# An earlier request for one weight block, and no meeting point between the recurrent mixer and the output products

## The reference, cut to what matters

```
h = rmsnorm(x, g_mix);  z = h @ w_in
q, k, v, f   = z's fox columns          # forgetting attention, 8 heads of 64
zr           = z's recurrent columns    # token shift, then a delta-rule recurrence, 8 heads of 64
zg           = z's gate columns, 2048
y_fox  = fox_attention(q, k, v, log_sigmoid(f))                    # [1024, 512]
y_rwkv = (group_norm(rwkv_scan(...)) + bonus) * g                  # [1024, 512]
merged = sigmoid(zg[:1024]) * (y_fox  @ w_o_fox)
       + sigmoid(zg[1024:]) * (y_rwkv @ w_o_rwkv)
x = x + merged @ w_out
h2 = rmsnorm(x, g_ffn); ... convolved, gated feed-forward of width 2816 ...
x = x + sigmoid(rmsnorm(x, g_ple) @ w_ple_gate) * (p @ w_ple_up)
```

## Time and profile before

| | |
|---|---|
| median of 3 runs | 4171.37 us (4163.51 to 4181.7) |
| the profiled execution | 4164.4 us, its span 4162.7 us |
| TensorE busy (matmul) | 3855.2 us, 93% |
| VectorE busy | 2273.4 us, 55% |
| ScalarE busy | 1195.5 us, 29% |
| GpSimd busy | 448.0 us, 11% |
| mean granted TensorE clock | 0.955 |

### The profile page before, as it was taken

One profiled execution on the slowest core, in us unless ns is written; L12 is line 12 of the kernel. 1 busy time (PEld: TensorE's weight loads), 2 busy tenths in 40 slices (PEclk: granted clock), 3 DMA queues, 4 the chain that ended last, 5 costly groups with the idle time before them and its releaser, 6 DMA issues. The chain is left out here.

```text
span 4162.7 us, 76117 instructions
## 1 busy us (share of the span) xinstructions
PE 3855.2 (93%) x33370; PEld 3166.3 (76%) x33370; DVE 2273.4 (55%) x3787; ACT 1195.5 (29%) x1698; POOL 448.0 (11%) x440
## 2 busy tenths in 40 slices
PE   6999969888999999999999999788788999999998
PEld 5888847777877888888798677566676788888887
DVE  4643335555434666766625333466554476666675
ACT  4221234433222433121401322243323321111123
POOL 0001102231000433000000000232311000000000
PEclk9999979998999999999999999888889999999999
DMA  5221130113112334422233422201004211111112
GB/s 182 83 64 49 48 112 6 33 31 128 51 56 86 107 107 137 167 100 73 90 121 117 144 76 86 80 23 59 23 30 155 91 51 41 51 43 59 41 61 81
DMA packets 230589, 327.11 MB, mean 79 GB/s; under 512 B 17372, under 2 KB 171740, under 8 KB 230132
## 3 DMA queue, kind: packets, MB, share of 16 engines
q1 hardware_dynamic: 201616, 259.52, 18.8%
q10 hardware_dynamic: 28644, 62.72, 3.9%
HBM read 239.66 MB, written 82.54 MB: 77 GB/s over the span
## 5 line engine op out<-in xcount | busy, mean ns | idle before, releaser
L471 PE MATMUL ps<-sb_a_h,sb_whi 128*128 128x512 f32 (+1 forms) x2336 | 930.8, 398 | 5.1 <-DVE sb_wlo L432 5.1
L473 PE MATMUL ps<-sb_a_h,sb_whi 128*128 128x512 f32 (+1 forms) x2336 | 914.3, 391 | 0.0
L472 PE MATMUL ps<-sb_a_h,sb_wlo 128*128 128x512 f32 (+1 forms) x2336 | 914.2, 391 | 0.0
L471 PEld LDWEIGHTS ps<-sb_a_h,sb_whi 128*128 128x128 f32 (+1 forms) x2336 | 440.8, 189 | 113.0 <-issue 15.7
L472 PEld LDWEIGHTS ps<-sb_a_h,sb_wlo 128*128 128x128 f32 (+1 forms) x2336 | 441.0, 189 | 94.9 <-issue 4.9
L473 PEld LDWEIGHTS ps<-sb_a_h,sb_whi 128*128 128x128 f32 (+1 forms) x2336 | 440.5, 189 | 94.4
L422 ACT ACTIVATE sb_whi<-sb_wraw 128x2048 fp32r<-128x2048 f32 (+2 forms) x129 | 233.2, 1808 | 765.4 <-PE ps L473 494.0
L677 DVE TENSOR_TENSOR sb_x<-sb_x,ps 128x512 f32<-128x512 f32 x480 | 314.8, 684 | 211.6 <-PE ps L473 197.3
L432 DVE TENSOR_TENSOR sb_wlo<-sb_wraw,sb_whi 128x2048 fp32r<-128x2048 f32 (+2 forms) x129 | 281.6, 2183 | 220.6 <-ACT sb_whi L422 200.9
L471 PE MATMUL ps<-sb_a_g,sb_whi 128*128 128x512 f32 x864 | 337.4, 391 | 11.5 <-DVE sb_x L677 10.5
L472 PE MATMUL ps<-sb_a_g,sb_wlo 128*128 128x512 f32 x864 | 336.3, 389 | 0.0
(11 more groups left out here) (599 smaller groups left out, 6754.3 us busy)
## 6 DMA issues: line engine op xcount, KB each, us to landing
sb_wraw<-w_in SPq DMA_DIRECT2D x33, 1024.0 KB, 5.3
sb_wraw<-w_ff SPq DMA_DIRECT2D x32, 1024.0 KB, 5.4
sb_wraw<-w_up SPq DMA_DIRECT2D x22, 1024.0 KB, 5.1
sb_wraw<-w_down SPq DMA_DIRECT2D x11, 1024.0 KB, 5.0
sb_wraw<-w_xkv SPq DMA_DIRECT2D x8, 1024.0 KB, 5.5
sb_wraw<-w_out SPq DMA_DIRECT2D x8, 1024.0 KB, 5.2
sb_b<-rw_d SPq DMA_DIRECT2D x16, 512.0 KB, 6.4
sb_b<-y SPq DMA_DIRECT2D x16, 512.0 KB, 5.8
```

The costliest lines, as they stand in the source:

```text
L471: e.matmul(o, wh[:, k, c], xh[:, sl], start=(k == 0), stop=False)
L472: e.matmul(o, wl[:, k, c], xh[:, sl], start=False, stop=False)
L473: m = e.matmul(o, wh[:, k, c], xl[:, sl], start=False, stop=(k == t.nk - 1))
```

## The change

In a4, SP asks for gate block 2 directly before the stores of p's product; before, it asked for it after them. It can do so as soon as the low part of p's weight block is made.

Between b2 and a5, the meeting is gone. Unit 7's result is no longer stored and loaded again. Columns 0 to 895 of the recurrent rows are loaded from `y2`; their last 128 columns (`newest`) are split directly from the buffer `ys[1]`, by one more instruction on ScalarE and one on VectorE, the latter ahead of VectorE's four others. In the place of the meeting stand single waits: on SP, for unit 7's last product, the last bonus, both store signals, and the last high part of the fox rows (`first_rows_cut`, the last L3501); on ScalarE, for the gate product of unit 7 and its last state update before row 4 is written. Tiles 5 to 8 take their banks from a ring of their own, (0, 1, 2, 3), and wait for one more low part. The gate loads use six existing semaphores (`s_o`), and the mixer's semaphores are given back one stage later.

```diff
@@ sp_a4 @@
                         next(sp_fox)
+                sp_load(e, gates[0].j + 2)
                 for t in ple:
                     e.wait_ge(*bk.emptied(t.key))
@@ sp_scan @@
                 yield from rest(12)
+                if i == 7:
+                    return
                 e.wait_ge(*bk.emptied(("rw_gate", i)))
@@ b2, and behind it @@
-            return o_tiles
+            return o_tiles, w4(ys[1])
...
-        o_tiles = b2()
-        o_first = [(t.key, bk.of[t.key]) for t in o_tiles[:4]]
-        next_phase()
-        bk.of.update(o_first)
-        stage_over(mixers)
-        merged, g_act, g_in = sig("gated_sum"), sig("gate_activated"), [dma_sig(f"gate_in{j}") for j in range(6)]
+        o_tiles, last_rows = b2()
+        first_rows_cut = lhi.last()
+        count_anew()
+        merged, g_act, g_in = sig("gated_sum"), sig("gate_activated"), s_o[:6]
@@ pe_a5 @@
-                pe_first(e, tiles[4:8], lambda k: hp(4 + k), llo.at)
+                pe_first(e, tiles[4:8], lambda k: hp(4 + k), lambda i: llo.at(i + 1), None, None, None, (0, 1, 2, 3))
                 for t in tiles[8:]:
                     pe_fm(e, t, lambda k: hp(4 * t.a + k))
-                pe_first(e, outs[:4], hp, lambda k: llo.at(4 + k))
+                pe_first(e, outs[:4], hp, lambda k: llo.at(5 + k))
@@ ve_a5 @@
+                e.wait_ge(*lhi.at(4))
+                e.tensor_tensor(newest(12), last_rows, newest(4).bitcast(F32), ALU.subtract).then_inc(*llo.up())
                 for k in range(4):
-                    e.wait_ge(*lhi.at(k))
-                    e.tensor_tensor(hp(4 + k)[1], raw(4 + k), hp(4 + k)[0].bitcast(F32), ALU.subtract).then_inc(*llo.up())
+                    e.tensor_tensor(hp(4 + k)[1][:, 0:896], raw(4 + k)[:, 0:896], hp(4 + k)[0][:, 0:896].bitcast(F32),
+                                    ALU.subtract).then_inc(*llo.up())
                     if k == 1:
                         ve_cut(e, tiles[0].j + 2)
@@ ac_a5 @@
                 for k in range(4):
                     e.wait_ge(*lp[k].at(0))
-                    e.activation(hp(4 + k)[0], raw(4 + k), ACT.Copy).then_inc(*lhi.up())
+                    if k == 3:
+                        e.wait_ge(*bk.filled(("rw_gate", 7)))
+                        e.wait_ge(*bk.emptied(("rw_k", 7, 1)))
+                    e.activation(hp(4 + k)[0][:, 0:896], raw(4 + k)[:, 0:896], ACT.Copy).then_inc(*lhi.up())
                     if k == 1:
                         ac_cut(e, tiles[0].j + 2)
+                e.wait_ge(*bk.emptied(("rw_gate", 7)))
+                e.activation(newest(4), last_rows, ACT.Copy).then_inc(*lhi.up())
@@ a5 @@
+            def newest(row):
+                return HH[:, row * T:(row + 4) * T].rearrange("p (k t) -> p k t", k=4)[:, :, 896:1024]
@@ sp_a5 @@
+                e.wait_ge(*bk.filled(("rw_o", 7, 1)))
+                e.wait_ge(*rw_bonus.last())
+                for r in rw_out:
+                    e.wait_ge(*r.last())
+                e.wait_ge(*first_rows_cut)
                 for k in range(4):
-                    e.dma_start(raw(4 + k), S["y2"][(4 + k) * 128:(5 + k) * 128, :]).then_inc(*lp[k].up())
+                    e.dma_start(raw(4 + k)[:, 0:896], S["y2"][(4 + k) * 128:(5 + k) * 128, 0:896]).then_inc(*lp[k].up())
@@ behind a5 @@
         count_anew()
+        stage_over(mixers)
```

More of the change, by code:

```diff
@@ L4198, in ve_a5 @@
                 for k in range(8):
-                    e.wait_ge(*lhi.at(4 + k))
+                    e.wait_ge(*lhi.at(5 + k))
                     e.tensor_tensor(hp(k)[1], xk(k), hp(k)[0].bitcast(F32), ALU.subtract).then_inc(*llo.up())
@@ L4226, in ac_a5 @@
                     e.activation(hp(k)[0], xk(k), ACT.Copy).then_inc(*lhi.up())
-                e.wait_ge(*llo.at(11))
+                e.wait_ge(*llo.at(12))
                 e.dma_start(xv, S["x_spill"].rearrange("(k p) t -> p k t", p=128)).then_inc(*x_back.up())
```

## The result

The changed kernel takes 4144.99 us in the median of 8 runs (4133.13 to 4159.86), against 4171.99 of the kernel before, timed beside it (8 runs, 4159.84 to 4181.7): ratio 0.9943, interval [0.9925, 0.9961], so 16 to 31 us less. The forecast was 4155.7 us, 15.7 less, with a range of 4145 to 4168: the median lies at its lower edge, 27.0 us under the kernel before. The profiled execution took 4133.13 us.

A forecast was written before the change was run, and what follows sets the result against it. TensorE, at work 93% of the span, was taken as the bound, so only its idle time counted: 5.8 + 8.8 + 1.1 = 15.7 us off the median 4171.37 gives 4155.7 us, range 4145 to 4168.

The forecast's parts named there:

- The request: At L3328's wait for ScalarE's square: asking for gate block 2 earlier starts TensorE 5.8 us sooner.
- SP has 17.7 us of cover: SP's earlier request waits for p's weight cut (L432); the stores behind it have 17.7 us to spare.
- The clock at the first gap: After L3328's remaining 2.7 us wait, TensorE's clock may stay up: half of 2.2 us counted, 1.1.
- The meeting: Before tiles 5 to 8 (L721): earlier row loads and free banks gain 8.8 us, leaving 3.7 of wait.
- The clock at the second gap: After L721's remaining 3.7 us wait, the clock falls as before (2.1 us); no gain counted.
- Rival 1: The clock stays up after both remaining waits, L3328 and L721: gain 18.9 us, 4152.5 us; chance 0.15.
- Rival 2: L3328's gain is lost in later fox steps or a later meeting: gain 8.8 us, 4162.6 us; chance 0.11.
- Rival 3: SP's row loads still wait for the fox products' end: nothing gained there, 4164.5 us; chance 0.07.
- Rival 4: Later tiles sit four banks back in the ring: 0.08 us lost on each of 296, 4179.4 us; chance 0.05.

The follow-up runs named there:

- changed_again: The changed kernel unaltered, timed and traced a second time: 4150.20 us, 0.9961 of the kernel before.
- before_again: The kernel before unaltered, under a second name: 4165.86 us, ratio 1.0003.
- early_only: The kernel before with only SP's earlier request for gate block 2, the meeting kept: 4150.89 us, 0.9955.
- cuts_ahead: The changed kernel with the weight block's cuts, then `newest`, ahead of the loaded rows on ScalarE and VectorE: 4141.20 us, 0.9939 of the kernel before.
- old_banks: The changed kernel with the usual ring of six banks for tiles 5 to 8: 4142.07 us, 0.9948 of the kernel before.
- early_again: The same kernel as early_only, timed and traced once more: 4154.74 us, 0.9975 of the kernel before.
- no_meeting_only: The changed kernel without the earlier request for gate block 2: 4158.31 us, 0.9973 of the kernel before.
- own_banks_only: The kernel before, its meeting kept, with only banks 0 to 3 for tiles 5 to 8: 4166.36 us, 0.9997.
- both_places: cuts_ahead with ScalarE's and VectorE's cuts of gate block 2 also moved from gate tile 1 to 3: 4133.52 us, 0.9913 of the kernel before.
- square_late_request: The kernel before, request still late, with ScalarE's first three fox steps ahead of its cut of gate block 2: 4159.56 us, 0.9985.

## Why the prediction was right, and where it fell short

The mechanism held at every link: 18.5 us at the two places in the first trace and 17.0 in the second (changed_again against before_again), where 15.7 were forecast; with what was lost behind place 2, 17.3 and 15.7. Both timings of the kernel contain these: 16 to 31, and 10 to 23 us. The median of the first timing, 27.0 us less, does not follow from the sum. It stands at the very edge of the range (4144.99 against 4145) and below the forecast's own 4149 to 4164; some 10 us of it came in stretches that the prediction did not count. That it was not further off is luck; the second timing, 4150.20 us, lies inside.

- *The request.* Forecast 5.8 us; the wait fell by 6.65. The step is mis-sized because ScalarE's last store issues, whose end at 2360.08 I took as fixed, carried a scatter of nearly 1 us. Where that stood in the trace again, the wait was 2.71 us, the forecast's 2.7. "SP has 17.7 us of cover" held: the stores kept their 28.10 us.
- *The clock at the first gap.* Counted half, 1.1 of 2.2. Six traces have a gap of this size. After 1.80 us the clock stayed at 1.00 in three of them (changed, early_only, cuts_ahead); it fell after 1.88 (changed_again), 1.96 (old_banks) and 2.71 us (early_again), each time for 3.2 to 3.4 us at the lower level, which costs 1.6 to 1.7. So the first pair of profiles had the whole 2.2 us, the second some 0.8 (a fall that cost 2.5 before and 1.7 after): the forecast's half happens to lie between these, by luck. The prediction went by the length of the gap, between 2.25 us that kept the clock and 3.17 that didn't; length alone doesn't order the cases. changed_again, its wait and the stretch behind it; then the wait of 3.43 us at the end of place 2 in no_meeting_only, which kept the clock, while behind the same wait it fell in the other thirteen traces:

```profile
2365.84 1.84 PE L3329 MATMUL ps<-sb_x,sb_consts 128*128 128x512 f32 x2 [1.88 <-ACT sb_x L3405]
```

```profile
2365.84:2369.24 3.40, 3.40 (x7) 2.02 (x8) 1.32 (x1) 1.93 (x2) 0.00 (x0) 0.54 0.84 276
```

```profile
3244.34 0.47 PE L721 MATMUL ps<-sb_a_h,sb_whi 128*128 128x512 f32 x1 [3.43 <-DVE sb_a_h L4202]
```

```profile
3244.34:3249.34 5.00, 5.00 (x22) 4.13 (x23) 5.00 (x5) 4.31 (x5) 0.00 (x0) 1.00 0.00 0
```

- *The meeting.* Forecast 8.8 us; the wait fell by 9.04, and the remaining one was 3.45 instead of 3.7. By the forecast's own distances from the first issue: ScalarE's fifth ends 9.1 us behind it (forecast 9.1), VectorE's cut 13.0 (13.2), TensorE starts at 13.0 (13.3). The low parts took 0.69 and 2.09 (0.7 and 2.2).
- *The clock at the second gap.* It fell, as said, but to 0.64 over 4.3 us where it had been 0.53 over 4.7, which gave 0.6 us not counted.
- *Rival 1* (both gaps keep the clock): the first did, the second not. *Rival 2* (given back later): the stretch between the places shows no wait that grew; the 1.2 us at L3368 and the 5.5 at L721 are as in every kernel. *Rival 3* (loads don't start early): refuted by 3112.67, right behind the last fox row. *Rival 4* (the ring of banks): from the end of place 2 to TensorE's 4.4 us wait for VectorE's L760 it is 837.5 or 837.6 us in ten of the traces, with the old ring (before, old_banks) and the new (changed, own_banks_only), so nothing per tile where 0.053 would decide. The others are no_meeting_only (837.1), which kept the clock behind the 3.43 us wait, and the three with the cuts ahead (838.5), where the fall there lasted longer: 0.55 over 6 us in cuts_ahead, 0.72 before.
- *Behind the last wait.* The sum had no term there, since no instruction changes; the clock took 1.2 us back.
- *The range* rested on executions that differ by more than any term is in doubt, and that was the right reason. The other 12.5 us between the two profiles (31.0 - 18.5 = 5.4 + 8.3 - 1.2) lie in unchanged stretches, largely by the clock: the whole stretch up to 2030 us, which no kernel here alters, took 2021.8 to 2039.7 us over the fourteen traces, and 2030.2 and 2039.7 in two of the very same kernel (before, before_again).

**Left open.** Over the twelve comparisons with an edit in them the timed gain is on average 4.4 us above what the two places show (both_places 36.3 against 25.8, early_only 18.8 against 8.6, changed_again 16.3 against 17.2, own_banks_only 1.3 against 4.7; the places against the mean of before and before_again), and 5.0 if the stretch behind place 2 is counted too. Kernels timed together share their runs of the kernel before, so these are not twelve independent numbers. Between the places lies the mixer; that stretch took 732.0 to 753.5 us, of it 129 to 191 us at the clock's lower level (worked out from the granted clock of windows of 5 us: twice what it lacks to 1.00, times their length). The six traces with both edits average 738.7 us, the eight others 747.4, but the two groups overlap (749.0 in old_banks, 738.2 in square_late_request). The edits alone timed 18.8 and 11.3 us less, together 23.8, so the times hold nothing for the rival that the two do more than their sum. No experiment parted an effect of the edits in the mixer's stretch from scatter, and I know of no way in which they would reach that stretch.

## What to carry to other kernels

Ask of each weight block's cut in an engine's order who needs it and when: a cut for a later tile stands like a gate before everything behind it, on every engine that shares in it, and moving it a few instructions down gave more here (about 10 us) than bringing its data early (6 to 9). Where rows come back from a mixer, put the work that is ready ahead of the work that is loaded, and give the tiles behind it banks that are free. For effects of a few us compare distances between two fixed waits of one engine, not spans, repeat them, and read the clock inside them too; and never forecast from the duration of one instruction in one execution.

## What the runs showed of the hardware

The same instructions differ by 17.9 us over the first 2030 us and by up to 21.5 over the 740 around the mixer, largely by the granted clock: up to 2030 us, some 158 to 206 us at the lower level. Whether the clock falls behind a short wait isn't told by the wait's length: it fell behind 1.88 and 1.96 us and stayed behind 2.25 and, in one trace of fourteen, behind 3.43. The Trainium skill (TensorE: Matmul & The Clock Gate, "What's actually happening") says that how many matmuls run at the lower clock varies between runs of one kernel; the traces agree, with 183 and 206 us in before and before_again.

A pair of store issues on ScalarE took 1.70 to 1.72 us in 3 traces and 0.88 or 0.89 in 11, with SP's request for a weight block 0.02 to 0.03 us behind its first in all fourteen. In before and early_again that request itself took 1.66 and 1.67 us, and 0.44 in the changed kernel. That both were long together says they share something; what it was in those three is not settled. The Trainium skill (DMA: Bandwidth & Descriptors, "Issuing engines are not separate DMA queues") says that transfers from several engines run on the same 16 and only the issue is saved by spreading them; here, in 3 of 14, not even the issue was (both took 1.7 us side by side; 0.88 and 0.44 one after the other would be 1.32).
